# Hybrid diffusion step on one core: the low parts of the expert weights made by VectorE alone instead of VectorE and GpSimd

## What is computed

```python
aff = softmax(xt @ w_router)                 # 640 x 16
gate, idx = top_k(aff.T, cap)                # 80 rows for each expert: 64 latent, 16 context
xe = xt[idx]
hg = einsum("ecd,edf->ecf", xe, w_g)         # w_g, w_u, w_d: 16 x 1024 x 1024 each, float32
hu = einsum("ecd,edf->ecf", xe, w_u)
y = einsum("ecf,efd->ecd", silu(hg) * hu, w_d) * gate
out = zeros.at[idx].add(y)                   # rows added into the residual stream
```

## Time and profile before

| | |
|---|---|
| median of three executions | 3039.09 us (3035.56 to 3041.82) |
| the profiled execution | 3039.95 us, its span 3038.1 us |
| TensorE matmul busy | 2699.2 us (89%) |
| VectorE busy | 1934.6 us (64%) |
| ScalarE busy | 1579.7 us (52%) |
| GpSimd busy | 869.8 us (29%), 509.0 us of it low parts (194) |
| read from memory | 568.88 MB, 196 GB/s over the span |
| expert stages | about 1010 to 1590 us and 2420 to 3000 us |

### The profile page before, as it was taken

How to read it: one execution, slowest core, us unless ns; L and a number is a source line. 1 busy time by engine, 2 the same in 40 slices (tenths; PEclk the granted TensorE clock), 3 DMA queues, 4 the chain that set the end, 5 groups by cost and what they waited for, 6 DMA issues and landing times.

```text
span 3038.1 us, 40777 instructions
## 1 busy us (share of the span) xinstructions
PE 2699.2 (89%) x13616; PEld 1916.1 (63%) x13616; DVE 1934.6 (64%) x2879; ACT 1579.7 (52%) x2282; POOL 869.8 (29%) x529
## 2 busy tenths in 40 slices
PE   6879999999995899999987999999999499999994
PEld 1248777777774565655657777777777356666562
DVE  6864356545337788888875346653435688888884
ACT  5543344333322677777763444433422377777774
POOL 0003000212121455555541200031122155555553
PEclk8879999999998999999998999999999799999997
DMA  9842011111232899999993211121233399999996
GB/s 334 322 141 87 28 39 56 49 51 54 99 104 108 291 365 356 364 357 359 359 340 109 72 32 35 35 77 35 63 117 127 132 351 365 366 361 364 361 357 222
DMA packets 191609, 595.91 MB, mean 196 GB/s; under 512 B 23008, under 2 KB 33054, under 8 KB 191478
## 3 DMA queue, kind: packets, MB, share of 16 engines
q1 hardware_dynamic: 172726, 529.76, 48.1%
q0 software_dynamic: 18640, 64.20, 7.1%
q10 hardware_dynamic: 112, 0.23, 0.0%
HBM read 568.88 MB, written 25.23 MB: 196 GB/s over the span
## 4 chain that ended last, share of the span: by engine, by line
PE 54%; issue 17%; DVE 9%; POOL 8%; DMA 6%; ACT 5%; POOLq 0%; SPq 0%; ACTq 0%; DVEq 0%
PE bank L447 14%; PE bank L449 13%; PE bank L448 12%; POOL low L1891 6%; PE bank L816 4%; PE bank L788 4%; DMA ring<-in_w_e_up 3%; ACT high L1002 2%; PE bank L806 2%; DVE low L1304 2%; POOL x_resid L1906 1%; DMA ring<-in_w_mod 1%; POOL U L1884 1%; PE bank L619 1%; PE bank L620 1%
## 5 line engine op out<-in xcount | busy, mean ns | idle before, releaser
L1002 ACT ACTIVATE high<-ring 128x1024 fp32r<-128x1024 f32 (+1 forms) x1012 | 1058.9, 1052 | 520.4 <-PE bank L449 279.5
L1708 DVE TENSOR_TENSOR low<-ring,high 128x1024 fp32r<-128x1024 f32 (+1 forms) x564 | 838.6, 1522 | 191.0 <-ACT high L1002 189.8
L1891 POOL TENSOR_TENSOR low<-ring,high 128x1024 fp32r<-128x1024 f32 (+1 forms) x194 | 509.0, 2624 | 595.7 <-ACT high L1002 580.3
L447 PE MATMUL bank<-high,hT_high 128*128 128x512 f32 (+2 forms) x1280 | 519.7, 406 | 25.7 <-ACT sigr L1088 13.6
L449 PE MATMUL bank<-high,hT_low 128*128 128x512 f32 (+2 forms) x1280 | 485.4, 379 | 0.0
L448 PE MATMUL bank<-low,hT_high 128*128 128x512 f32 (+2 forms) x1280 | 484.0, 378 | 0.0
L447 PE MATMUL bank<-high,xeT_high 128*80 128x512 f32 x1024 | 411.6, 402 | 32.0 <-POOL low L1891 29.7
L448 PE MATMUL bank<-low,xeT_high 128*80 128x512 f32 x1024 | 402.8, 393 | 0.0
L449 PE MATMUL bank<-high,xeT_low 128*80 128x512 f32 x1024 | 401.9, 392 | 0.0
L1304 DVE TENSOR_TENSOR low<-ring,high 128x1024 fp32r<-128x1024 f32 (+2 forms) x254 | 303.5, 1222 | 139.2 <-ACT high L1002 137.8
L1189 ACT ACTIVATE att<-bank,st 128x640 f32<-128x640 f32 (+3 forms) x200 | 136.5, 683 | 351.4 <-DVE st L1563 256.8
(11 more groups left out here) (238 smaller groups left out, 3324.5 us busy)
## 6 DMA issues: line engine op xcount, KB each, us to landing
ring<-in_w_e_down SPq DMA_DIRECT2D x260, 512.0 KB, 5.2
ring<-in_w_e_gate SPq DMA_DIRECT2D x256, 512.0 KB, 6.0
ring<-in_w_e_up SPq DMA_DIRECT2D x256, 512.0 KB, 6.9
ring<-in_w_mod SPq DMA_DIRECT2D x96, 512.0 KB, 6.3
ring<-in_w_gate SPq DMA_DIRECT2D x64, 512.0 KB, 3.8
ring<-in_w_in SPq DMA_DIRECT2D x24, 512.0 KB, 5.0
ring<-in_w_branch SPq DMA_DIRECT2D x16, 512.0 KB, 4.3
ring<-in_w_out SPq DMA_DIRECT2D x16, 512.0 KB, 5.0
```

What stands on the lines that cost most here:

```text
L447: nc.tensor.matmul(out, lhs[0], rhs_high, start=start, stop=False)
L1002: A(high[:, g % HIGH, :, 0:w], ring[:, g % RING, :, 0:w], ACT.Copy).then_inc(high_done, 1)
L1708: V.tensor_tensor(low[:, (g + HIGH) % RING, :, 0:w], ring[:, (g + HIGH) % RING, :, 0:w], high[:, g % HIGH, :, 0:w].bitcast(F32), ALU.subtr ...
L1891: G.tensor_tensor(low[:, g % RING, :, 0:w], ring[:, g % RING, :, 0:w], high[:, g % HIGH, :, 0:w].bitcast(F32), ALU.subtract).then_inc(low_ ...
```

## The change

GpSimd makes no low parts. `by_pool`, its two tables and the semaphore `low_pool` go; VectorE makes the low part at every step j, and TensorE waits for `low_dve` alone. What stays on GpSimd in the expert stage is the gather, the scatter and the wait for its landing, in this order.

```diff
-def by_pool(g):
-
-    l, c = divmod(g - CH_MOD, CH_LAYER)
-    return g >= CH_MOD and g % 4 == 3 and (c >= CH_DENSE or (c < HIGH and l > 0))
...
             def split_done(g, i=None):
-                s, n = (low_pool, LOW_POOL[g]) if by_pool(g) else (low_dve, LOW_DVE[g])
-                if i is None:
-                    pe.wait_ge(s, n)
-                else:
-                    pe.wait_ge(s, i * (2 * CH_EXP // 4 * (1 if by_pool(g) else 3)) + n)
+                pe.wait_ge(low_dve, g + 1 if i is None else i * (2 * CH_EXP) + (g + 1))
...
             def split_low(g):
-                if by_pool(g):
-                    return
                 dve.wait_ge(high_done, g + 1)
...
-                        if not by_pool(g + HIGH):
-                            dve.wait_ge(high_done, i * (2 * CH_EXP) + (g + HIGH + 1))
-                            w = NEXT_W if last and l + 1 < L and j >= 4 * NQ - HIGH else NW
-                            V.tensor_tensor(low[:, (g + HIGH) % RING, :, 0:w], ring[:, (g + HIGH) % RING, :, 0:w],
-                                            high[:, g % HIGH, :, 0:w].bitcast(F32), ALU.subtract).then_inc(low_dve, 1)
+                        dve.wait_ge(high_done, i * (2 * CH_EXP) + (g + HIGH + 1))
+                        w = NEXT_W if last and l + 1 < L and j >= 4 * NQ - HIGH else NW
+                        V.tensor_tensor(low[:, (g + HIGH) % RING, :, 0:w], ring[:, (g + HIGH) % RING, :, 0:w],
+                                        high[:, g % HIGH, :, 0:w].bitcast(F32), ALU.subtract).then_inc(low_dve, 1)
...
-                def expert(e, i, last=False, rows=True):
+                def expert(e, i, rows=True):
                     n_exp = i * 2 + (NE * l + e)
-                    at = CH_GATE0 + e * CH_EXP
-                    for j in range(2 * HIGH + HIGH, (4 if last else 6) * NQ + 1, HIGH):
-                        split_low(g0 + at + j, i, NEXT_W if last and l + 1 < L and j == 4 * NQ else NW)
-                        if j == 4 * HIGH and rows:
-
-                            gather(e, i * 2 + (NE * l + e + 3))
+                    if rows:
+                        gather(e, i * 2 + (NE * l + e + 3))
                     pool.wait_ge(y_ready, n_exp + 2)
                     pool.sem_inc(pool_held, 1)
                     pool.indirect_dma_start(out=x_dram, out_offset=bass.IndirectOffsetOnAxis(ap=idx_s[:, e, 0:1], axis=0),
                                             in_=ybuf[0:CAP, e, :], in_offset=None, compute_op=ALU.add).then_inc(y_out, 16)
-                    if not last:
-                        for j in range(HIGH, 2 * HIGH + 1, HIGH):
-                            split_low(g0 + at + CH_EXP + j, i)
-
                     pool.wait_ge(y_out, n_exp * 16 + 16)
                     pool.sem_inc(added, 1)
-                split_low(g0)
                 gather(0, NE * l + 1)
                 gather(1, NE * l + 2)
                 pool.wait_ge(gate2_in, 32 * (l + 1))
-                for j in range(HIGH, CH_GATE0 + 2 * HIGH + 1, HIGH):
-                    split_low(g0 + j)
```

More of the change, by code:

```diff
@@ L222, in width_of @@
     return NW
-def by_pool(g):
-    l, c = divmod(g - CH_MOD, CH_LAYER)
-    return g >= CH_MOD and g % 4 == 3 and (c >= CH_DENSE or (c < HIGH and l > 0))
-LOW_POOL = [sum(map(by_pool, range(g + 1))) for g in range(N_CHUNKS + HIGH)]
-LOW_DVE = [g + 1 - LOW_POOL[g] for g in range(N_CHUNKS + HIGH)]
 def hybrid_step(nc, x_prompt, x_sample, cache_diff_k, cache_diff_v, cache_na_k, cache_na_v, cache_swa_k,
@@ L372, in hybrid_step @@
         ring_used = sem("ring_used")
-        high_done, low_dve, low_pool = sem("high_done"), sem("low_dve"), sem("low_pool")
+        high_done, low_dve = sem("high_done"), sem("low_dve")
         small_in = sem("small_in")
@@ L1885, in gather @@
                                             in_offset=bass.IndirectOffsetOnAxis(ap=idx_g[:, b, 0:1], axis=0)).then_inc(xe_in[b], 16)
[L1887 to L1894, removed]
-                def expert(e, i, last=False, rows=True):
-                    n_exp = i * 2 + (NE * l + e)
-                    at = CH_GATE0 + e * CH_EXP
-                    for j in range(2 * HIGH + HIGH, (4 if last else 6) * NQ + 1, HIGH):
-                        split_low(g0 + at + j, i, NEXT_W if last and l + 1 < L and j == 4 * NQ else NW)
-                        if j == 4 * HIGH and rows:
-                            gather(e, i * 2 + (NE * l + e + 3))
+                def expert(e, i, rows=True):
+                    n_exp = i * 2 + (NE * l + e)
+                    if rows:
+                        gather(e, i * 2 + (NE * l + e + 3))
                     pool.wait_ge(y_ready, n_exp + 2)
@@ L1924, in _ @@
                 expert(0, LOOPED, rows=False)
-                expert(1, LOOPED, last=True, rows=False)
+                expert(1, LOOPED, rows=False)
             pool.dma_start(gfin_b, g_final.rearrange("(a n) -> a n", a=1).broadcast_to([P, D])).then_inc(gfin_in, 16)
```

## The result

| | before | after |
|---|---|---|
| median of 13 executions each | 3037.94 us | 3050.39 us |
| ratio, 95% interval | | 1.0042 (1.0028 to 1.0057) |
| the profiled execution | 3039.95 us | 3041.13 us, its span 3039.3 us |

One execution of before took 10862.77 us; it is counted in the median and left out of the ratio.

What follows compares the result with a forecast made beforehand. TensorE and DMA were both taken as nearly full in the expert stages, with TensorE stalled on low parts. -46.8 - 12.6 + 1.0 = -58.4 us, less 13 us for weights, gave -45 us: 2994 us, range 2979 to 3029.

Steps and rivals of the forecast that it cites:

- Step 1: In the expert stages, weight-load waits on GpSimd's low parts (L1891) go: 23.6 + 23.2 = 46.8 us gained.
- Step 2: At the start of each down matrix, the wait for hidT_low shrinks: 0.45 x 28 = 12.6 us gained.
- Step 3: In the expert stage, GpSimd's gather goes out 15 us earlier; with 17 us of slack its lateness costs nothing.
- Step 4: VectorE's low of chunk 3 precedes y_half: free with punctual weights; if 1 us late, chunk 4's low is late next.
- Step 5: Outside the loop, before the router and at a stage's end, VectorE's changed order costs together +1.0 us.
- The weights: In the expert stages, slow stretches of weight transfers give back 0.8 us a pair, between 0 and 3.2: 13 us.
- A: DMA becomes the bound in the expert stages, gain 8 to 30 us: 3009 to 3031 us; chance 0.25.
- B: VectorE's 24 lows an expert become the bound, deciding at 1.35 us each: slower, 3079 or 3180 us; chance 0.05.
- C: Nothing to measure: expert-stage stalls move one for one to late weights, 3033 to 3045 us; chance 0.06.

Runs made afterwards that it cites:

- half loads: Expert loads bring half of each row, same element counts: on the change 2979.8 us; on the kernel before 2969.91 us, then 2995.45 us with GpSimd reading two tiles.
- the order mended: Change with late gather, hidT_high and hidT_low ahead of chunk 16's high and low parts: 2998.11 us; with y_half also ahead of the last low: 2985.2 us.

## Why the prediction was wrong

**Step 1, the waits on L1891 (-46.8 us): right that they go, wrong in what they were worth.** The low parts take 1.22 us and L1891 is gone. But the step priced these waits as GpSimd's lateness, while its own sum said that with GpSimd 3.9 of 4.1 us are used up, that is, no stall. The half loads confirm that sum: once weights are on time, 0.5 us of matmul waits for GpSimd's lows are left in layer 1. As the size of these stalls the 46.8 us were not far off, since half loads alone take them away and give 41.8 us. But it was lateness of the weights, which no faster low part removes. ScalarE's 78 us of waits for DMA in that stretch were the row to read beside it, and the prediction didn't.

**Step 2, hidT_low (-12.6 us): a gain became a loss.** The chain became shorter as worked out (0.42 us a time), and with weights on time the matmuls' wait falls by just that, from 0.75 to 0.35 us. In the real kernel it mostly starts, or goes on, when the late weight comes and not when TensorE releases the buffer, and the wait rose from 0.75 to 1.45 us in layer 1 (20.3 in 14) and 1.7 in layer 2 (23.9 in 14), 44.2 us in all against 21.0. The bounds, 0 to -21, held no loss.

**Step 3, the gather costs nothing: wrong by 26.7 us, and this is what turned the sign.** With the gather held back the same change is 12.9 us faster than the kernel before. It went out 9 to 12 us behind the scatter's issue, some 13 us earlier than before (15 foretold). Its rows arrived in time for TensorE, as foretold. What it did to the weights was left to the part on them, as 0.8 us a pair given back with the sentence that it goes "to a time when the queue is deep". In fact it made the down matrix late instead of the up matrix. The kernel before is indifferent to that (3038.9 us), the change isn't. That the stall at chunk 11 makes the difference is argued from the timelines; no run puts such a stall into the change.

**Step 4, y_half: right, and conditional as put.** "where they are 1 us late, this low is what is late next" came true: moving it gives 13 us, but only after the hidden rows are out of the way. **Step 5** is within what can't be told here.

**The weights (+13 us): by far too small.** The low parts' move gives 15.6 us with weights on time and 12.9 with the real ones and the gather held back; the gather's move takes that back twice over. So of the 58.4 us some 43 were not there to be had even with weights on time: they had been late weights all along, for which the half loads measure 41.8. DMA's mean stayed at 359 GB/s, where 373 to 378 were foretold; 375 came only with the order mended and the gather late.

**The rivals.** A was nearest in its cause, late weights, and its sign, too, was wrong: it treated 360 GB/s as a rate, while 346 to 384 GB/s come out of the same bytes when only the order of instructions changes. B is refuted: 1.22 us a low is under its 1.35. A loss came all the same, by a mechanism that the prediction had no rival for: a late weight in front of an operand that doesn't need it. C's thought, stalls that move one for one, describes the profiled execution best (29.1 to 31.0 us).

Left open: what part of the gather's remaining 12 to 20 us is its traffic and what the order of other operations, and whether a gather between the two places would be better still; neither was tried.

## What to carry to other kernels

A wait names the engine that came last, not the one that was late: follow the named engine's own waits back, here ScalarE's for DMA, before giving the named engine's work to another. Where engines work through a list in order, look for operands that stand behind a load they don't need; an earlier stall may be hiding them, and whatever removes that stall can expose them. A change that moves one item often moves a second one along (here a gather); try the two apart, each also on the kernel before, since their effects need not add up.

## What the runs showed of the hardware

- The rate of the weights goes with how steadily slots come free: 346 GB/s with long stalls, 359 in the change, 375 and 384 with the order mended and the gather late, 393 with one product instead of three, all with the same loads. From 1050 to 1500 us two issues lay over 2 us apart 36, 28, 13 and 5 times in the first four.
- GpSimd's subtraction of 128x1024 took 1.89 us when both operands were one tile and 2.4 us with two (means, beside VectorE, 1.97 and 2.70).
- VectorE's subtraction took 1.53 us on average beside GpSimd's and 1.22 without, with full loads and with half loads alike: in the kernel before, DMA traffic had no part in its length.
- A scatter's issue on GpSimd took 2.23 us on average in the expert stage before and 2.88 in after, 1.39 us at the stage's end, where VectorE was idle. Of the 15 issues in layer 1 of after, 13 ended 0.11 to 0.23 us behind the end of one of VectorE's low parts. The gather's issue got shorter, 1.75 to 1.36 us on average: 0.92 us where it began ahead of a low part or with it, up to 2.24 us where it began during one. The Trainium skill (SBUF — State Buffer, the box on VectorE blocking DMA) says, of VectorE's two-port modes, that GpSimd can't write descriptors while VectorE holds the shared port. The trace agrees in direction for the scatter, here beside subtractions with two inputs; no run priced it by itself.
